# Turning attention probabilities by a DRAM exchange and VectorE stream transposes instead of TensorE, steps 32 to 53

## The reference

```python
def mixer_b(q, k, v, rel_table):
    ...
    logits = jnp.einsum('bcqhd,bckhd->bhcqk', qc.astype(jnp.float32),
                        kb.astype(jnp.float32)) * SCALE
    ...
    logits = logits + bias[:, None]
    logits = jnp.where(valid[:, None, :], logits, NEG)
    p = jax.nn.softmax(logits, axis=-1)
    out = jnp.einsum('bhcqk,bckhd->bcqhd', p.astype(vb.dtype), vb)
    return out.reshape(b, s, B_W)
```

## Time and profile before

| | us |
|---|---|
| median of 3 runs | 1033.59 |
| span of the profiled execution (first to last instruction) | 1031.9 |
| PE busy | 1023.0 (99%) |
| DVE busy | 770.9 (75%) |
| ACT busy | 470.5 (46%) |
| POOL busy | 219.7 (21%) |
| mean granted TensorE clock | 0.999 of full |

### The profile page before, as it was taken

How to read it: one execution, slowest core, us unless ns; L and a number is a source line. 1 busy time by engine, 2 the same in 40 slices (tenths; PEclk the granted TensorE clock), 3 DMA queues, 4 the chain that set the end, 5 groups by cost and what they waited for, 6 DMA issues and landing times.

```text
span 1031.9 us, 15795 instructions
## 1 busy us (share of the span) xinstructions
PE 1023.0 (99%) x5525; PEld 851.0 (82%) x5525; DVE 770.9 (75%) x1506; ACT 470.5 (46%) x978; POOL 219.7 (21%) x218
## 2 busy tenths in 40 slices
PE   9999999999999999999999999999999999999997
PEld 8899887788778888878888888888888888888886
DVE  4955677867688578888988788786444777778997
ACT  6632355545477567836221221311344445454562
POOL 5200000000000003148675674761100000000000
PEclk9999999999999999999999999999999999999999
DMA  9835442111071474045444434446777733454344
GB/s 202 222 98 136 108 134 77 42 47 37 11 225 43 123 188 159 21 143 212 171 167 155 163 134 152 163 144 225 243 243 242 229 103 92 143 194 142 93 142 164
DMA packets 135071, 147.92 MB, mean 143 GB/s; under 512 B 72248, under 2 KB 85440, under 8 KB 132944
## 3 DMA queue, kind: packets, MB, share of 16 engines
q1 hardware_dynamic: 133920, 146.68, 45.7%
q10 hardware_dynamic: 688, 0.20, 0.1%
q0 software_dynamic: 384, 0.04, 0.0%
HBM read 103.65 MB, written 47.49 MB: 146 GB/s over the span
## 4 chain that ended last, share of the span: by engine, by line
PE 94%; DVE 3%; issue 1%; DMA 1%; ACT 0%; POOL 0%; DVEq 0%; ACTq 0%; POOLq 0%
PE ps L2242 27%; PE ps L2244 27%; PE ps L2243 27%; PE ps L2451 3%; PE ps L2465 3%; PE ps L2432 2%; PE ps L2376 1%; DVE wc_lo L1918 1%; PE ps L2411 1%; PE ps L2584 1%; PE ps L2586 1%; PE ps L2572 1%; DMA up_raw<-in_w_up 1%; DVE b_lo L1907 1%; PE ps L2254 0%
## 5 line engine op out<-in xcount | busy, mean ns | idle before, releaser
L2242 PE MATMUL ps<-b_hi,wc_hi 128*128 128x512 f32 x448 | 174.6, 390 | 0.5 <-DVE wc_lo L1918 0.5
L2243 PE MATMUL ps<-tm_lo,sm_hi 128*128 128x512 f32 (+1 forms) x450 | 174.6, 388 | 0.0
L2244 PE MATMUL ps<-tm_hi,sm_lo 128*128 128x512 f32 (+1 forms) x450 | 174.6, 388 | 0.0
L2242 PE MATMUL ps<-tm_hi,sm_hi 128*128 128x512 f32 (+1 forms) x450 | 174.6, 388 | 0.0
L2244 PE MATMUL ps<-b_hi,wc_lo 128*128 128x512 f32 x448 | 174.3, 389 | 0.0
L2243 PE MATMUL ps<-b_lo,wc_hi 128*128 128x512 f32 x448 | 174.3, 389 | 0.0
L1485 ACT ACTIVATE sm_hi<-sm_raw 128x512 fp32r<-128x512 f32 x112 | 70.7, 631 | 161.8 <-DMA sm_raw<-u_matrices 161.8
L2146 DVE TENSOR_TENSOR sm_lo<-sm_raw,sm_hi 128x512 fp32r<-128x512 f32 x112 | 77.4, 691 | 77.9 <-ACT sm_hi L1485 77.3
L2242 PEld LDWEIGHTS ps<-b_hi,wc_hi 128*128 128x128 f32 x448 | 84.1, 188 | 18.3 <-DVE wc_lo L1918 0.9
L2242 PEld LDWEIGHTS ps<-tm_hi,sm_hi 128*128 128x128 f32 x450 | 84.5, 188 | 17.6
L2244 PEld LDWEIGHTS ps<-tm_hi,sm_lo 128*128 128x128 f32 x450 | 84.5, 188 | 17.4
(11 more groups left out here) (261 smaller groups left out, 2063.2 us busy)
## 6 DMA issues: line engine op xcount, KB each, us to landing
u_matrices<-stage SPq DMA_DIRECT2D x112, 256.0 KB, 2.0
sm_raw<-u_matrices SPq DMA_DIRECT2D x112, 256.0 KB, 2.6
up_raw<-in_w_up SPq DMA_DIRECT2D x16, 1024.0 KB, 5.0
w<-in_w_down SPq DMA_DIRECT2D x64, 256.0 KB, 3.8
w_raw<-in_w_in SPq DMA_DIRECT2D x8, 512.0 KB, 3.5
xr<-in_x SPq DMA_DIRECT2D x8, 512.0 KB, 4.3
x_rows<-xr SPq DMA_DIRECT2D x8, 512.0 KB, 4.1
xf<-x_rows SPq DMA_DIRECT2D x8, 512.0 KB, 3.5
```

The costliest lines, as they stand in the source:

```text
L2242: pe.matmul(out, w_hi_, x_hi_, start=start, stop=False)
L2243: pe.matmul(out, w_hi_, x_lo_, start=False, stop=False)
L2244: return pe.matmul(out, w_lo_, x_hi_, start=False, stop=stop)
```

## The change

For steps 32 to 53 (`turned_b`) PE no longer turns the probabilities: `chunks_of` is empty there. Instead:

- ACT `normalize` multiplies by the reciprocal and writes the result in another order to a second half of `prob_b` (`stored_probs`). `prob_b` has one slot for each head now, so DVE's `scores` of the next step wait for it.
- SP `exchange_step` stores each head's block rows to DRAM (`pb_dram`) and loads them back into one of three buffers `turn_in`, so that each 32x32 block is where its transposed stands: 2 stores and 2 loads a step, each with a wait. The loads of `load_fill` and `load_bias` stand between the steps' exchanges.
- DVE `turn_probs` transposes within the 32x32 blocks from `turn_in` into `probT_b`, two steps after the scores. `invert` is the reciprocal alone.
- PE `weigh` reads the turned probabilities as four runs of 32 columns and writes PSUM with a step of 4 elements (`"p (j c) -> p c j"`). It comes one pair of steps later: steps n-4 and n-3 stand in odd step n. Its bank is 7 or 5, and the late fill halves alternate between banks 6 and 4, each with the wait for the half before the last (`s_et`) in place of the last.
- From step 54 on all is as before, but for the weighing of steps 51, 52 and 53 and the turning of 52 and 53, which fall there.

```diff
-    if paired(n) and nk <= 2:
-        return [(0, 2 * nk, nk == 1)]
+    if turned_b(n):
+        return []
     if nk < B_KEYS:
         return [(0, nk, True), (nk, nk, False)]
-    return [(0, 4, True), (4, 4, True), (8, 2, n >= LATE - 1)]
+    return [(0, 4, True), (4, 4, True), (8, 2, True)]
...
 def fill_bank(m):
-    return 4 + m % 2 if m < SINGLE else 4
-
+    return 4 + m % 2 if m < SINGLE else 6 - m % 2 * 2
...
+        turn_in = (sb("turn_in0", 204, [P, B_KEYS, P]), v_tok[:, :, 0:P], mix[:, 1, :, 3])
...
         def prob_of(n, hh):
-            return prob_b[:, 2 * (n % 2) + hh]
+            return prob_b[:, hh if turned_b(n) else 2 * (n % 2) + hh]
+
+        def stored_probs(n, hh):
+
+            return prob_b[:, 2 + hh, 0:keys_of(n) * P]
...
+            def exchange_step(n):
+
+                m = keys_of(n) * 32
+                for hh in range(2):
+                    q = turn_number(n, hh)
+                    sp.wait_ge(s_pb, pb0 + q + 1)
+                    sp.dma_start(pb_dram[q, 0:512 * m].rearrange("(a p m) -> p a m", a=4, m=m),
+                                 stored_probs(n, hh).rearrange("p (a m) -> p a m", m=m)).then_inc(s_pst[hh], 16)
+                for hh in range(2):
+                    q = turn_number(n, hh)
+                    sp.wait_ge(s_pst[hh], pst0[hh] + 16 * (n - A_STEPS + 1))
+                    if q == 0:
+                        sp.wait_ge(s_pv, A_STEPS)
+                    elif q >= 3:
+                        sp.wait_ge(s_tb, tb0 + q - 2)
+                    sp.dma_start(turn_in[q % 3][:, 0:keys_of(n)],
+                                 pb_dram[q, 0:512 * m].rearrange("(p k n) -> p k n", p=P, n=P)).then_inc(s_pld[q % 3], 16)
...
+            for n in range(A_STEPS, LATE):
+                exchange_step(n)
+                if n == A_STEPS:
+                    load_bias(5)
+                elif n % T == T - 1:
+                    sp.wait_ge(s_nm, 2 * n + 2)
+                    load_bias(n // T + 2)
+                elif n % 4 == 1 and n // 4 + 2 - A_STEPS // 4 + 4 < FILL_TILES:
+                    load_fill(n // 4 + 2 - A_STEPS // 4 + 4)
...
+            def normalize(n, hh):
+                at = 2 * (n % 2) + hh
+                act.wait_ge(s_ri, 2 * n + hh + 1)
+                if n > A_STEPS:
+                    act.wait_ge(s_pst[hh], pst0[hh] + 16 * (n - A_STEPS))
+                nc.scalar.activation(stored_probs(n, hh).rearrange("p (a k i) -> p k a i", a=4, i=32),
+                                     prob_of(n, hh)[:, first_column(n):].rearrange("p (k a i) -> p k a i", a=4, i=32),
+                                     ACT.Copy, scale=rinv[0][:, at:at + 1]).then_inc(s_pb, 1)
...
+            for n in range(A_STEPS, LATE):
...
+                for hh in range(2):
+                    exp(n, hh)
...
+                for hh in range(2):
+                    normalize(n, hh)
+                tiles_hi(halves_done(n - 1))
+                splits(n)
...
+                    if A_STEPS < n <= LATE:
+                        dve.wait_ge(s_pb, pb0 + turn_number(n - 1, hh) + 1)
...
+            def turn_probs(n, hh):
+
+                q = turn_number(n, hh)
+                dve.wait_ge(s_pld[q % 3], pld0[q % 3] + 16 * (q // 3 + 1))
+                dve.wait_ge(s_pv, n - 1)
+                nk = keys_of(n)
+                nc.vector.transpose(blocks(prob_t(n, hh)[:, 0:nk * P]), turn_in[q % 3][:, 0:nk]).then_inc(s_tb, 1)
...
+            for n in range(A_STEPS, LATE):
                 done = halves_done(n - 1)
-
                 take(done)
-                if n < STEPS and not (paired(n) and n % 2):
+                scores(n)
+                for hh in range(2):
+                    if n >= A_STEPS + 2:
+                        turn_probs(n - 2, hh)
+                    invert(n, hh)
+                take_low(done)
+                splits(n)
...
+            for n in range(LATE, STEPS + 1):
...
+                if n < LATE + 2:
+                    for hh in range(2):
+                        turn_probs(n - 2, hh)
...
-                    pe.wait_ge(s_et, scaled_when(m - (2 if m < SINGLE else 1)))
+                    pe.wait_ge(s_et, scaled_when(m - (1 if m == SINGLE else 2)))
...
             def weigh(n):
                 p, t = n // T, n % T
                 nk = keys_of(n)
-                pe.wait_ge(s_pta, copies(n, True))
-                if copies(n, False):
-                    pe.wait_ge(s_ptd, copies(n, False))
+                if turned_b(n):
+                    pe.wait_ge(s_tb, tb0 + turn_number(n, 1) + 1)
...
                 for k in range(nk):
                     for hh in range(2):
-                        last = pe.matmul(ps[64 * hh:64 * hh + 64, 7, (t % 4) * P:(t % 4) * P + P],
-                                         v_tok[:, t + 1 - nk + k, at + 64 * hh:at + 64 * hh + 64],
-                                         prob_t(n, hh)[:, k * P:(k + 1) * P], start=(k == 0), stop=(k == nk - 1))
+                        out_ = ps[64 * hh:64 * hh + 64, weigh_bank(n), (t % 4) * P:(t % 4) * P + P]
+                        if turned_b(n):
+                            out_ = out_.rearrange("p (j c) -> p c j", c=4)
+                            probs = turned_query_blocks(n, hh)[:, k]
+                        else:
+                            probs = prob_t(n, hh)[:, k * P:(k + 1) * P]
+                        last = pe.matmul(out_, v_tok[:, t + 1 - nk + k, at + 64 * hh:at + 64 * hh + 64], probs,
...
+            for n in range(A_STEPS, LATE):
...
+                elif n % 2:
+                    if n > A_STEPS + 3:
+                        weigh(n - 4)
+                    weigh(n - 3)
+                first, end = filled(n - 1), filled(n)
                 for m in range(first, end):
-                    if m == first + 2 and n % T == 3:
-                        transposes(n, 0)
-                        transposes(n, 1)
...
-                        transposes(n - 1, 2)
...
                     fill(m)
...
+            for n in range(LATE, STEPS + 1):
+                if n < STEPS:
+                    scores(n)
+                for c in range(len(chunks_of(n - 1))):
+                    transposes(n - 1, c)
+                if n < LATE + 3:
+                    weigh(n - 3)
+                if n >= LATE + 2:
                     weigh(n - 2)
```

More of the change, by code:

```diff
@@ L1812, in _ @@
                 splits(n + 3)
[L1814 removed]
+            for n in range(A_STEPS, LATE):
                 done = halves_done(n - 1)
                 take(done)
[L1818 removed]
+                scores(n)
+                for hh in range(2):
+                    if n >= A_STEPS + 2:
+                        turn_probs(n - 2, hh)
[3 more added lines that the diff above has]
+            for n in range(LATE, STEPS + 1):
+                done = halves_done(n - 1)
+                take(done)
+                if n < STEPS:
                     scores(n)
@@ L2491, in _ @@
                     fill(m)
-            for n in range(A_STEPS, STEPS + 1):
-                first, end = min(filled(n - 1), 8 * HALVES), filled(min(n, STEPS - 1))
-                if A_STEPS + 2 < n < LATE and n % 2:
-                    weigh(n - 3)
-                    weigh(n - 2)
-                if n < STEPS and not (paired(n) and n % 2):
+            for n in range(A_STEPS, LATE):
+                if not (paired(n) and n % 2):
                     scores(n)
```

163 lines of the change are left out of this document (75 added, 88 removed).

## The result

The changed kernel takes 1049.77 us (median of 4 runs, 1049.51 to 1053.28), the kernel before beside it 1033.7 (1033.16 to 1033.89): ratio 1.0165, 95% interval 1.0151 to 1.018. The prediction was 1023.0, range 1016.5 to 1037, with 0.17 for slower. Direction and range are both wrong.

What follows compares the result with a forecast made beforehand. PE was taken as the bound. Gains of 16.0 (transposes) and 0.97 (moved weighing) less 2.0 (DVE's lag) and 4.35 (late stretch) gave 10.6 us, from the median 1033.59 to 1023.0; range 1016.5 to 1037.

Steps and rivals of the forecast that it cites:

- What leaves PE: PE ahead of step 54: 150 transposes removed gain 16.0 us, and the moved weighing of step 51 gains 0.97.
- the lag: Steps 32 to 53: DVE runs behind what PE needs, 0.7 us a round over 2.75 rounds, 2 us lost.
- The spread PSUM write: Weighing on PE, writing PSUM one element in four: taken as costing nothing, with 19.2 us as upper bound.
- Rival 1: The spread write slows PE's weighing; at double length 1042.2 us. Chance 0.15 for a loss above 10 us, 0.05 for smaller.
- DVE's and ACT's pieces: Five-block steps: 0.85 us for a DVE stream transpose of 640 columns, about 0.7 for ACT's product of 640 columns.
- The late stretch: From step 54's scores to step 57's: about 14.9 us in place of 10.55, a loss of 4.35 us.
- So it is hidden by the two steps, with 0.3 us or more to spare: Exchange, steps 32 to 53: store and load at 3.1 us each finish before the transpose two steps on; nothing charged.
- SP's other transfers ... also hidden: Transfers behind each step's loads: fill weights asked some 4 us later but needed about 9 us later, so no cost.
- Rival 2: DVE and the exchange become the bound: 0.8 us more for each of ten five-block steps, 8 us, 1031. Chance 0.15.
- the steps counted on to catch up: Steps of 1 to 4 key blocks, whose scores take a half or less, let DVE catch up with PE.
- The clock: A granted clock below full behind the late waits would add time that no row showed; no size given.

## Why the prediction was wrong, step by step

- **What leaves PE: right.** Without transfers the four stages sum to 116.46 us (37.12, 37.72, 27.26, 14.36) against 128.30. Ahead of step 54 that is 15.65 us gained, where the prediction's terms give 16.0 + 0.97 - 2.0 = 14.97. The difference lies in the lag: without transfers PE waits 0.9 us for DVE's scores ahead of step 54, where 2 were charged.
- **The spread PSUM write: right to take nothing.** Step 41 of the changed kernel weighs steps 37 and 38. This is the weighing of step 37, ten matmuls with two records each; that of step 38 follows behind the wait of 3.48 us:

```profile
217.72 1.31 PE L2555 MATMUL ps<-probT_b,v_tok 128*64 128x128 f32 x20
```

  20 records in 1.31 us, the duration that the earlier trace rows has for 20 with a plain write. Rival 1 is false. The Trainium skill ("Advanced Engine Details and Errata", Memory Cachelines) says that such a write slows matmuls significantly; the trace does not agree for this form (float32, 32 columns in a run on the moving side, one element in four written).
- **DVE's and ACT's pieces: right.** A transpose of 640 columns, and ACT's product:

```profile
L1794 DVE STREAM_TRANSPOSE probT_b<-turn_in 128x640 f32<-128x640 f32 x6 | 5.0, 840 | 2.1 <-DMA turn_in<-prob_step_tiles 2.0
```
```profile
L1246 ACT ACTIVATE prob_b<-prob_b,small 128x640 f32<-128x640 f32 x16 | 12.9, 826 | 10.9 <-DMA prob_step_tiles<-prob_b 10.6
```

  0.84 for 0.85, and 0.83 for "about 0.7", too little by 0.13.
- **The late stretch: right in size without transfers** (14.36 for 14.9), with some luck, since the 14.36 hold a granted clock of 0.88 that the prediction had at full. In the changed kernel it was 21.65, with the granted clock at 0.61.
- **"So it is hidden by the two steps, with 0.3 us or more to spare": this step failed.** The runs showed in its place that the exchange costs 28.2 us, and that 19.1 of them go when a load needn't wait for its own store. Three things were missing. First, both transfers were put in at 3.1 us, which the earlier trace rows show for the bias tables' loads. In the kernel the medians are 4.6 for the store and 3.3 for the load, and by these the chain still fits: 4.3 + 4.6 + 3.3 = 12.2 us, where the prediction has the second head's transpose start at 12.9. But with the 6.95 us of step 38 between store and load it ends at 14.6, 1.7 too late. The sum took one time for all steps where the late ones decide. Second, the sentence followed the load to its reader and not the slot back to its writer: the next product waits for the landing as well, on an engine on which `tile_hi` and `wf_hi` stand behind it. Alone this is worth 3.3 us. Third, SP's queue was taken as a list of times and not as a line that stops: it waits for each landing, and the next store stands behind that. The runs don't price this apart from the first.
- **"SP's other transfers ... also hidden": failed.** They were not late for their own readers, but they stood ahead of the stores. Taking them out of SP's queue gave 10.5 us.
- **Rival 2 was the right mechanism, at a third of its price or less.** It priced 0.8 us for each of ten five-block steps, 8 in all, where the exchange cost 28.2. Its sign came: DVE waited 12.1 us for loads, 0.55 for each of 22 steps. But the largest wait, ACT's 31.3 us for its slot, isn't in it. Measured, the round from 40 to 48 is 12.92 us longer than without transfers, and the steps counted on to catch up are the worst: the scores of steps 40 and 42 are 14.38 us apart (213.89 and 228.27), without transfers 9.14, before 10.86. A step with few keys asks for little work of DVE but still waits for the landing of the big step before it.
- **The clock: named and not priced.** The sentence that it could add "what no row here shows" was right. PE in step 55 of the changed kernel:

```profile
306.64 2.37 PE L2532 MATMUL ps<-ident,prob_b 128*128 128x128 f32 x10 [2.23 <-DVE prob_b L1807]
308.94 2.40 PE L2555 MATMUL ps<-probT_b,v_tok 128*64 128x128 f32 x20
```

  Ten transposes take 2.37 us where the earlier trace rows have 1.31, 20 weighing records 2.40 for 1.31: the lower of the clock's two levels, 1.2 GHz. By stretches that follow a wait of PE:

```profile
202.00:207.00 5.00, 4.90 (x22) 3.90 (x23) 4.94 (x16) 4.24 (x10) 0.00 (x0) 0.66 0.77 228
222.00:227.00 5.00, 4.49 (x28) 3.65 (x29) 2.57 (x6) 2.37 (x4) 0.00 (x0) 0.68 0.72 228
252.00:257.00 5.00, 5.00 (x21) 3.93 (x18) 4.49 (x15) 4.03 (x9) 0.00 (x0) 0.50 0.82 261
302.00:312.00 10.00, 7.32 (x48) 6.28 (x48) 6.90 (x17) 4.53 (x12) 0.00 (x0) 0.51 0.81 231
```

  The last one includes further waits. Two thirds of a microsecond were paid again in clock for each microsecond waited (12.7 against 18.7), as the difference of two profiled executions.

Not settled: what the last 2.5 us are that stay when no load from step 37 on waits for its store, if they are more than spread. And why moving the weights to ScalarE's queue gives 10.5 us beside the whole chain but costs 4.0 without it. In the second case a load of 320 KB into `turn_in` took 5.0 us in the median, against 4.1. A version that turns three steps behind the scores, and not two, should give the chain more time, which no run shows; it needs further buffers in PE's and DVE's order and wasn't tried.

## What to carry to other kernels

When work goes from an engine to an exchange through DRAM, price the chain and not the transfers: store, landing, load, landing, each at the time it takes beside its neighbours in the queue, with both ends followed, to the reader of the load and back to the writer of the stored buffer, and with whatever stands behind each waiting instruction. Price the slowest step beside the median one. A reserve of 0.3 us was no cover here: a gain of 12 became a loss of 16. And take the whole chain out in an experiment before you cure its parts, since a cure alone may only show which wait comes next (the free slot gave 3.3 us of 28.2), and cures together need not add (the weights and the third slot).

## What the runs showed of the hardware

- The landing of a store of 320 KB in 512 pieces depends on its neighbours: 2.7 us where the loads were asked later (transposes last), 4.6 in the changed kernel, both in the median; and right behind 512 KB of weights 6.95 and 7.05 until the load behind it could be asked, 6.26 and 4.61 with these weights on the other queue. Pieces of 2560 B in place of 640 B gave only 4.2.
- A second issuing queue didn't bring the transfers back to quiet times. With the stores on ScalarE's queue they still took 3.8 us, and the weights there 4.4 and up to 6.3 in the median. The Trainium skill ("DMA: Bandwidth & Descriptors", Issuing engines are not separate DMA queues) says that all issuing engines feed the same DMA engines; the runs fit that and don't test it apart. What a second queue did give is order: stores that don't stand behind SP's waits (6.5 us), or weights that don't stand ahead of the stores (10.5).
- Matmuls that write PSUM one float32 in four ran at the pace of contiguous ones (1.31 us for 20 records of 128 columns, before and now).
- Waits of PE of 2.36, 3.48 and 2.40 us (up to 202.10, 222.51 and 251.46) were followed by stretches with a granted clock of 0.66, 0.68 and 0.50, with PE busy for 4.90, 4.49 and 5.00 of 5 us. Behind the wait of 1.49 us up to 194.18 it stayed at 1.00.
